# Gate and up products of an expert mixture in column bands, with the activations turned on VectorE

## The reference, cut to what matters

```
def moe_ffn(h, comb, wg, wu, wd):
    out = jnp.zeros_like(h)
    for e in range(N_EXPERTS):
        ye = (jax.nn.silu(h @ wg[e]) * (h @ wu[e])) @ wd[e]
        out = out + comb[:, e:e + 1].astype(h.dtype) * ye
    return out
```

## Time and profile before

| | us |
|---|---|
| median of three runs | 1065.74 |
| the profiled execution, in all | 1060.38 |
| its span, first to last instruction | 1058.6 |
| TensorE matmul busy | 987.4 |
| TensorE weight load busy | 751.7 |
| VectorE busy | 378.1 |
| ScalarE busy | 234.0 |
| DMA | 238.03 MB, mean 225 GB/s |

### The profile page before, as it was taken

How to read it: one execution, slowest core, us unless ns; L and a number is a source line. 1 busy time by engine, 2 the same in 40 slices (tenths; PEclk the granted TensorE clock), 3 DMA queues, 4 the chain that set the end, 5 groups by cost and what they waited for, 6 DMA issues and landing times.

```text
span 1058.6 us, 20482 instructions
## 1 busy us (share of the span) xinstructions
PE 987.4 (93%) x8640; PEld 751.7 (71%) x8640; DVE 378.1 (36%) x831; ACT 234.0 (22%) x465; POOL 145.5 (14%) x230
## 2 busy tenths in 40 slices
PE   4999999999989899999999999999799999999960
PEld 2667676676756566666666677666699999999960
DVE  3121235666436985666441610223011010010106
ACT  2130222332352322322241100014111011110003
POOL 0000233342000542243200000002000000000004
PEclk8999999999999999999999999998899999999995
DMA  9853346457354565656534533432749999999944
GB/s 381 306 197 119 122 157 226 142 199 244 126 185 160 184 223 200 199 183 213 180 126 146 202 122 123 153 119 93 266 173 402 396 411 397 395 414 399 403 167 141
DMA packets 47444, 238.03 MB, mean 225 GB/s; under 512 B 6832, under 2 KB 11472, under 8 KB 24080
## 3 DMA queue, kind: packets, MB, share of 16 engines
q1 hardware_dynamic: 45568, 231.63, 58.8%
q0 software_dynamic: 1472, 5.24, 1.5%
q10 hardware_dynamic: 336, 0.20, 0.1%
HBM read 212.31 MB, written 24.75 MB: 224 GB/s over the span
## 4 chain that ended last, share of the span: by engine, by line
PE 87%; DVE 3%; ACT 3%; issue 3%; DMA 2%; POOL 1%; SPq 0%; ACTq 0%; POOLq 0%; DVEq 0%
PE pjB L811 14%; PE pjA L811 14%; PE states L1364 11%; PE pjA L1202 7%; PE pjB L1202 7%; PE states L1367 5%; PE pjA L1364 3%; PE pjB L1364 3%; PE pjB L1367 2%; PE pjA L1367 1%; PE states L820 1%; PE bank L1166 1%; PE bank L935 1%; PE states L1181 1%; PE states L935 1%
## 5 line engine op out<-in xcount | busy, mean ns | idle before, releaser
L811 PE MATMUL pjB<-hF,ring 128*128 128x320 f32 x608 | 173.4, 439 | 0.0
L811 PE MATMUL pjA<-hF,ring 128*128 128x320 f32 x608 | 171.9, 436 | 0.5 <-ACT regA L1553 0.5
L1367 PE MATMUL states<-ring,oF 128*32 128x384 f32 x1392 | 154.8, 491 | 0.0
L1364 PE MATMUL states<-ring,oF 128*32 128x128 f32 x1392 | 154.8, 273 | 0.0
L1364 PEld LDWEIGHTS states<-ring,oF 128*32 128x32 f32 x1392 | 150.7, 110 | 2.6 <-issue 2.6
L811 PEld LDWEIGHTS pjB<-hF,ring 128*128 128x128 f32 x608 | 114.3, 192 | 49.2 <-issue 5.7
L811 PEld LDWEIGHTS pjA<-hF,ring 128*128 128x128 f32 x608 | 113.2, 190 | 50.7 <-issue 7.0
L2486 DVE TENSOR_TENSOR oF<-oF,states 128x384 f32<-128x384 f32 x16 | 8.9, 555 | 168.6 <-PE states L1367 168.6
L2243 DVE TENSOR_TENSOR G<-G 128x320 f32<-128x320 f32 x32 | 46.6, 1495 | 0.0
L1863 POOL TENSOR_TENSOR G<-regA,G 128x128 f32<-128x128 f32 (+1 forms) x32 | 19.0, 595 | 196.4 <-ACT G L1609 196.4
L1367 PE MATMUL pjB<-ring,hF 128*32 128x384 f32 x384 | 44.7, 491 | 0.0
(11 more groups left out here) (476 smaller groups left out, 1444.1 us busy)
## 6 DMA issues: line engine op xcount, KB each, us to landing
ring<-in_w SPq DMA_DIRECT2D x171, 1024.0 KB, 6.9
G<-in_ss SPq DMA_DIRECT2D x16, 512.0 KB, 4.0
out_ss_new<-G SPq DMA_DIRECT2D x16, 512.0 KB, 2.8
G<-csd SPq DMA_DIRECT2D x16, 320.0 KB, 3.5
yd<-hF SPq DMA_DIRECT2D x16, 288.0 KB, 6.0
G<-in_sg SPq DMA_DIRECT2D x4, 1024.0 KB, 6.4
out_sg_new<-G SPq DMA_DIRECT2D x16, 256.0 KB, 2.9
rF<-in_w SPq DMA_DIRECT2D x2, 1024.0 KB, 9.3
```

Source lines behind the costliest of these rows:

```text
L811: mm = pe.matmul(pj[g % 2][:, 0:T], w[:, k, half * P:half * P + P], hF[:, k, :], start=(k == 0), stop=(k == KT - 1))
L1364: pe.matmul(bank[CAP:P, c * P:(c + 1) * P], rows(c, True), w[:, WIDE:512], start=first and c == 0, stop=last, tile_position=(0, CAP), skip ...
L1367: mm = pe.matmul(bank[QUAD * c:QUAD * c + QUAD, 0:WIDE], rows(c, False), w[:, 0:WIDE], start=first, stop=last, tile_position=(0, QUAD * c) ...
```

## The change

Gate and up use a new helper, `banded`. Each step of k has twelve products instead of six: for each block c of 32 rows and each column group q, the moving operand is the 32 weight columns 32q to 32q + 31 of each of the four runs of 128, 128 columns in four runs of 32. A bank now holds, in the 32 partitions of group q, the three blocks of rows side by side, each with its 128 features of band q. Turned in blocks of 32 by 32, this gives features on all 128 partitions, block k of 128 features for block c of rows at columns 128c + 32k. So `turn_act` goes, and VectorE's `turned` is one `transpose` from `actE` to `actT`, right behind the multiplication. `actT` is doubled, one half for odd and one for even experts, and is written as soon as the down of two experts before is done. `down` is as it was, but for where it finds its rows. VectorE's multiplication of the next expert waits for that transpose instead of the turn on TensorE.

```diff
-        actT = hF_[:, 4 * WIDE:5 * WIDE].rearrange("p (k c) -> p k c", k=BLOCKS)
+        actT = hF_[:, 4 * WIDE:6 * WIDE].rearrange("p (v c) -> p v c", v=2)
...
+            def banded(bank, rows, w, first, last):
+
+                w_ = w.rearrange("p (k q f) -> p q k f", q=4, f=QUAD)
+                for c in range(BLOCKS):
+                    for q in range(4):
+                        mm = pe.matmul(bank[QUAD * q:QUAD * q + QUAD, c * P:(c + 1) * P], rows(c), w_[:, q],
+                                       start=first and c == 0, stop=last, tile_position=(0, QUAD * q), skip_group_check=True)
                 return mm
...
-                            mm = tiled(b[2 + part], lambda c, tail: he[:, 4 * half + k, QUAD * c:QUAD * c + QUAD],
+                            mm = banded(b[2 + part], lambda c: he[:, 4 * half + k, QUAD * c:QUAD * c + QUAD],
                                        w[:, k, :], half + k == 0, half == 1 and k == 3)
...
-            def down(e, back):
+            def down(e, back, v):
...
-                        mm = tiled(pj[h], lambda c, tail: actT[:, k, QUAD * c:QUAD * c + QUAD] if k < BLOCKS
-                                   else actT[:, c, CAP:P], w[:, k, :], k == 0, k == 3)
+                        mm = tiled(pj[h], lambda c: act_[:, c * P + k * QUAD:c * P + k * QUAD + QUAD], w[:, k, :], k == 0, k == 3)
...
-            def turn_act(e):
-
-                pe.wait_ge(s_eac, e + 1)
-                for k in range(BLOCKS):
-                    mm = pe.transpose(b[4][:, k * P:(k + 1) * P], actE[:, k * P:(k + 1) * P], ident)
-                mm.then_inc(s_rd, 1)
...
-                        down(e, 1)
-                    turn_act(e)
+                        down(e, 1, 1 - v)
...
-                        dve.wait_ge(s_rd, GH + PAIRS + e)
+                        dve.wait_ge(s_hev, XROWS // P + e)
                     dve.tensor_tensor(actE, sgE, b[3][:, 0:WIDE], ALU.mult).then_inc(s_eac, 1)
...
-                def turned(e, back):
-
-                    dve.wait_ge(s_rd, GH + PAIRS + 1 - back + e)
-                    if not (isinstance(e, int) and e == back):
-                        moe_used(dve, e, 5, back + 1)
-                    dve.tensor_copy(actT, b[4][:, 0:WIDE].rearrange("p (k c) -> p k c", k=BLOCKS)).then_inc(s_hev, 1)
+                def turned(e, v):
+
+                    dve.wait_ge(s_eac, e + 1)
+                    if not (isinstance(e, int) and e < 2):
+                        moe_used(dve, e, 5, 2)
+                    dve.transpose(actT[:, v], actE).then_inc(s_hev, 1)
```

More of the change, by code:

```diff
@@ L1363, in tiled @@
                 for c in range(BLOCKS):
-                    pe.matmul(bank[CAP:P, c * P:(c + 1) * P], rows(c, True), w[:, WIDE:512],
+                    pe.matmul(bank[CAP:P, c * P:(c + 1) * P], rows(c), w[:, WIDE:512],
                               start=first and c == 0, stop=last, tile_position=(0, CAP), skip_group_check=True)
                 for c in range(BLOCKS):
-                    mm = pe.matmul(bank[QUAD * c:QUAD * c + QUAD, 0:WIDE], rows(c, False), w[:, 0:WIDE],
+                    mm = pe.matmul(bank[QUAD * c:QUAD * c + QUAD, 0:WIDE], rows(c), w[:, 0:WIDE],
                                    start=first, stop=last, tile_position=(0, QUAD * c), skip_group_check=True)
+                return mm
+            def banded(bank, rows, w, first, last):
[4 more added lines that the diff above has]
+                                       start=first and c == 0, stop=last, tile_position=(0, QUAD * q), skip_group_check=True)
                 return mm
@@ L1379, in gate_up @@
                         for k in range(4):
-                            mm = tiled(b[2 + part], lambda c, tail: he[:, 4 * half + k, QUAD * c:QUAD * c + QUAD],
+                            mm = banded(b[2 + part], lambda c: he[:, 4 * half + k, QUAD * c:QUAD * c + QUAD],
                                        w[:, k, :], half + k == 0, half == 1 and k == 3)
                         mm.then_inc(s_used, 1)
-            def down(e, back):
+            def down(e, back, v):
                 pe.wait_ge(s_hev, XROWS // P + e - back + 1)
+                act_ = actT[:, v]
                 for h in range(2):
@@ L1416, in one @@
                     else:
-                        down(e, 1)
-                    turn_act(e)
+                        down(e, 1, 1 - v)
                 experts(pe, one)
-                down(E - 1, 0)
+                down(E - 1, 0, (E - 1) % 2)
             with pe.Else():
@@ L2479, in one @@
                 def one(e, v):
-                    if not (isinstance(e, int) and e == 0):
-                        turned(e, 1)
                     moe_used(dve, e, 3)
@@ L2489, in one @@
                             copy_tokens(t)
+                        turned(e, v)
                     else:
+                        turned(e, v)
                         y_half(e, 1 - v, 1)
-                def turned(e, back):
-                    dve.wait_ge(s_rd, GH + PAIRS + 1 - back + e)
-                    if not (isinstance(e, int) and e == back):
-                        moe_used(dve, e, 5, back + 1)
-                    dve.tensor_copy(actT, b[4][:, 0:WIDE].rearrange("p (k c) -> p k c", k=BLOCKS)).then_inc(s_hev, 1)
+                def turned(e, v):
[3 more added lines that the diff above has]
+                    dve.transpose(actT[:, v], actE).then_inc(s_hev, 1)
                 experts(dve, one)
-                turned(E - 1, 0)
                 y_half(E - 1, (E - 1) % 2, 0)
```

## The result

The changed kernel takes **1159.7 us** (median of four runs, 1153.9 to 1162.3) against 1064.7 (1060.3 to 1066.5) for the kernel before on the same chip: ratio 1.088, 95% interval 1.0855 to 1.0906. It is 95 us slower, where 6.6 were forecast, and outside the range of 1057 to 1090.

A forecast was written before the change was run, and what follows sets the result against it. TensorE was taken as the bound, DMA a close second. Turns at -13.9 and misses at 5 x 4.1 gave +6.6 us on the profiled 1060.4, so 1067.0, carried over to the median as 1072; range 1057 to 1090.

The forecast's parts named there:

- The turn, 13.9 us off TensorE: Expert loop, before down: removing the turning products saves 0.82 us 15 times plus 1.55 once, 13.9 us.
- A banded step costs 0 more; the transpose costs nothing: Gate and up: twelve products a step add 0 us; VectorE's transpose hides under 5.2 us of down products.
- The body does not stay: TensorE's expert loop: the body grows from 4.7 to 7.7 instruction packets and is not kept on the engine.
- rival (a): Expert loop: the body stays resident and the kernel gets faster, -7 of the 13.9, 1058.7 us; chance 0.31.
- A miss costs 4.1 us, five times: Expert loop's back-edge: TensorE idles 4.1 us at each of five, 12.5 to 20.5 us in all.
- Fetching falls behind: Gate and up: packets wanted each 3.5 us come 0.5 us late, three an expert, 24 us.
- rival (b): Expert stage: misses also cool TensorE, or instruction fetching falls behind; 1083 to 1105 us, about 1088 likely; chance 0.17.
- DMA gives an expert in 16.6 us: Expert loop's weight loads: 6.69 MB an expert at 404 GB/s take 16.6 us, a close second to TensorE.
- A cooled TensorE: Behind loop back-edges: half rate for 4 to 8 us costs 2 to 4 a miss, 10 to 20 in all.
- the likeliest case: Whole kernel: turns removed, five back-edge misses added, +6.6 us, 1072 us; chance 0.40.
- what would show it: Signs in the profile after, listed for each case, such as branches of some 4 us or gaps amid gate and up.

The follow-up runs named there:

- experiment 1: The changed kernel with gate and up back to the old six products a step, VectorE's transpose kept: 1051.3 us, ratio 0.987.
- experiment 3: The changed kernel with TensorE's loop over experts written out, the other engines keeping theirs: 1120.2 us, ratio 1.054.
- experiment 6: The changed kernel with each refill of the weight ring cut to a quarter: 1061.0 us with TensorE's expert loop written out, 1108.4 us with the loop kept.

## Why the prediction was wrong

Step by step, as it was put:

- **The turn, 13.9 us off TensorE.** Right: 0.85 us an expert in the pass, 12.9 in the median (experiment 1).
- **A banded step costs 0 more; the transpose costs nothing.** Right: 0.649 us a step; 0.578 us and nobody late for it.
- **The body does not stay.** Right, and the rival (a), chance 0.31, falls. At 250 instructions a packet the bodies that stayed are up to 6.2 packets and the ones that did not begin at 7.0, so the usable end lies between six and seven; where a body begins within its first packet was not varied. The Trainium skill (Runtime: NRT & Kernel Launch, Instruction fetch mechanics) gives TensorE 128 KiB, refilled in blocks of 16 KiB, and says of a taken branch that it waits for a fetch when its target is not in a window of two pages. The trace does not agree with two: bodies of 4.7 to 6.2 packets came back in 0.21 us. Nor does it bear out that all eight blocks' worth can be used: 7.0 packets did not stay.
- **A miss costs 4.1 us, five times.** The term mis-sized: the hole at the back-edge is 4.9, near it, but a miss as a whole is 7.8 us, since a second hole follows (2.3 us, up to 865.67) and half rate after both. 5 x 7.8 = 39 instead of 20.5.
- **"Fetching falls behind" left out of the sum.** This is the step that failed. The prediction had the number that should have warned it, a packet each 3.5 us in gate and up where the trace had shown one each 7, and priced it in rival (b) at 0.5 us a packet, chance 0.17. (Rival (b)'s own prices, 10 to 20 for the clock and 24 for the packets on top of the +7, add up to 1107 to 1117 if both come, not to the 1105 at which it ended.) Measured: a pass of two experts in straight code is 9.4 us longer (experiment 3 against 1), 4.7 an expert instead of 1.5. Over all 16 experts this would be 16 x 4.7 = 75 us, and with the back-edges 39 and the turns -13.9 it makes +100, against 95 in the medians and 102 in the profiled spans. Over the whole kernel straight code costs somewhat less than 75: the medians of experiments 3 and 1 are 68.9 us apart, the profiled spans 65.7.
- **Its cause** was missing too: I had looked at the fetch as if it were alone. It shares DMA with weights at some 340 to 420 GB/s, and experiment 6 shows that in straight code this decides: with the same 94 packets the kernel takes 59 us less when the weights' traffic is a quarter. Behind a back-edge it does not: there a miss costs as much with light traffic.
- **DMA gives an expert in 16.6 us**. Wrong, without bearing on the result: 404 GB/s was what TensorE asked for, not what DMA could give; 422 came when more was asked (experiment 1), and the later landing (9.4 us) cost nothing.
- **A cooled TensorE**, the other half of rival (b), takes part: the clock account gives up to 35 of the 116 us lost in the stage (102, and the 13.9 of the turns).

So the likeliest case had the sign and the mechanism at the branch, and missed the larger half of the loss. Of what would show it, "gaps amid gate and up", named for (b), is what the trace shows.

Left open: when the chip asks for the next packet. In straight code at some 335 GB/s a packet is often not there in time; how far ahead it is asked for no run here tells. Nor does any tell what TensorE waits for in the second hole behind a back-edge, when no DMA packet moves. Open also are some 10 us between the written-out kernel with light DMA (1061.0) and experiment 1 (1051.3), which ran on two chips; small holes and a pass longer by 1.1 us are what the traces show of them. I did not try a loop over single experts, whose body of some 970 instructions should stay.

## What to carry to other kernels

Count TensorE's instructions twice: those in a loop body against what is known to stay (here 1,560 did and 1,750 did not), and those per microsecond against what the fetch brings beside the kernel's own DMA traffic (a packet of 250 each 7 us was free, one each 4 was not). Work taken off an engine by splitting its products is paid for per instruction, so look first for the form that widens them. Where a rival's own number says that a resource is asked for at twice the rate ever shown, its price belongs in the sum, with a wide range, and not beside it.

## What was not expected of the hardware

- A branch back to code that did not stay costs 7.8 to 9.2 us a time, of which the branch itself is 4.0 to 5.8; the rest is a second hole and half rate. Lighter DMA shortens the branch but not the whole: the second hole is 2.3 us at either traffic, and no DMA packet moves in it.
- The edge is sharp: 0.21 us a branch at 1,560 instructions, 5.7 at 1,750.
- In straight code instruction packets come late beside weight traffic: 45.7 us of holes at 335 GB/s, 4.5 at 127, with the same number of packets.
- One core moved 422 GB/s over 150 us, and TensorE waited for none of it.
- Moving float32 data in four or eight runs of 32 columns streams as fast as contiguous data, and a VectorE transpose of 128 x 384 in 32 by 32 blocks takes 0.58 us, as long as a copy of the same size (0.56).
